# Hymba block on one core: three products of an accumulator in a row in the feature-major projection

## What is computed

```python
h = rms_norm(x, g_mix[l])
p = h @ w_in[l]
aq, ak, av, mq, mk, mv, mo, mi, mf = jnp.split(p, split_idx, axis=-1)
...
qk = jax.nn.silu(causal_dwconv(jnp.concatenate([mq, mk], axis=-1), conv_qk[l]))
...
gates = jnp.concatenate([mi, mf], axis=-1) + b_gates[l]
```

## Time and profile before

| | us |
|---|---|
| median of three runs | 1000.84 |
| lowest and highest run | 1000.76, 1000.9 |
| profiled execution | 1005.44 |
| its span, first to last instruction | 1003.7 |
| TensorE busy in it | 991.8 (99%) |
| VectorE, ScalarE, GpSimd busy | 635.1, 422.7, 668.4 |
| mean granted TensorE clock | 0.995 |

### The profile page before, as it was taken

The page is one execution under the profiler, slowest core; times in us unless marked ns, Lnnn a source line. Parts: engine busy times, 40 slices in busy tenths (PEclk is TensorE's granted clock), DMA queues, the critical chain, the costliest instruction groups (busy, mean ns, idle before and its releaser), DMA issues.

```text
span 1003.7 us, 13162 instructions
## 1 busy us (share of the span) xinstructions
PE 991.8 (99%) x4862; PEld 822.5 (82%) x4862; DVE 635.1 (63%) x777; ACT 422.7 (42%) x868; POOL 668.4 (67%) x529
## 2 busy tenths in 40 slices
PE   9899999999999999999999999999999999999998
PEld 7697788888888888888888888888888888888887
DVE  5259224558862677876748577774748586674585
ACT  6533135547750657524334352434334252433440
POOL 0238056726675516996887786887878788787792
PEclk9999999999999999999999999999999999999999
DMA  8823112141032002112112112112112112211213
GB/s 307 190 75 104 42 43 64 54 147 33 23 126 63 22 11 74 53 42 84 43 42 84 42 43 85 43 42 77 50 42 70 57 42 60 67 42 49 82 59 137
DMA packets 74423, 70.69 MB, mean 70 GB/s; under 512 B 6520, under 2 KB 54776, under 8 KB 74360
## 3 DMA queue, kind: packets, MB, share of 16 engines
q1 hardware_dynamic: 72296, 69.36, 22.6%
q10 hardware_dynamic: 2064, 0.50, 0.3%
HBM read 65.14 MB, written 4.21 MB: 69 GB/s over the span
## 4 chain that ended last, share of the span: by engine, by line
PE 87%; DVE 5%; DMA 3%; SPq 3%; ACT 1%; issue 1%; DVEq 0%; ACTq 0%
PE banks L833 27%; PE banks L835 27%; PE banks L834 27%; DVE qkT L1776 2%; DMA x_in<-in_x 1%; SPq L577 1%; DMA rstd_rows<-rstd 1%; PE banks L1030 1%; PE banks L846 1%; PE banks L927 1%; PE banks L1005 1%; DVE qkT L1774 1%; ACT prob L1541 1%; PE banks L992 1%; DMA rstd_b<-rstd_rows 1%
## 5 line engine op out<-in xcount | busy, mean ns | idle before, releaser
L763 POOL TENSOR_TENSOR wr_lo<-wr_raw,wr_hi 128x512 fp32r<-128x512 f32 x231 | 319.1, 1412 | 27.3 <-ACT wr_hi L1356 22.2
L757 POOL TENSOR_TENSOR wr_raw<-wr_raw,wr_raw 128x512 f32<-128x512 f32 x132 | 193.4, 1469 | 132.2 <-PE banks L835 75.8
L833 PE MATMUL banks<-hf_hi,wr_hi 128*128 128x512 f32 x616 | 240.2, 390 | 0.0
L835 PE MATMUL banks<-hf_hi,wr_lo 128*128 128x512 f32 x616 | 240.0, 390 | 0.0
L834 PE MATMUL banks<-hf_lo,wr_hi 128*128 128x512 f32 x616 | 239.9, 389 | 0.0
L1356 ACT ACTIVATE wr_hi<-wr_raw 128x512 fp32r<-128x512 f32 x231 | 136.7, 625 | 164.8 <-POOL wr_raw L757 107.7
L2177 DVE TENSOR_TENSOR x<-banks,x 128x1024 f32<-128x1024 f32 x138 | 168.8, 1224 | 51.5 <-PE banks L835 35.2
L833 PE MATMUL banks<-w_hi,actT_hi 128*128 128x512 f32 (+1 forms) x384 | 147.9, 385 | 0.0
L835 PE MATMUL banks<-w_hi,actT_lo 128*128 128x512 f32 (+1 forms) x384 | 144.2, 375 | 0.0
L834 PE MATMUL banks<-w_lo,actT_hi 128*128 128x512 f32 (+1 forms) x384 | 144.1, 375 | 0.0
L833 PEld LDWEIGHTS banks<-hf_hi,wr_hi 128*128 128x128 f32 x616 | 115.7, 188 | 24.3 <-issue 0.4
(11 more groups left out here) (205 smaller groups left out, 1201.4 us busy)
## 6 DMA issues: line engine op xcount, KB each, us to landing
wr_raw<-in_w_up SPq DMA_DIRECT2D x46, 256.0 KB, 3.4
wr_raw<-in_w_gate SPq DMA_DIRECT2D x44, 256.0 KB, 3.3
wr_raw<-in_w_down SPq DMA_DIRECT2D x44, 256.0 KB, 3.2
w_raw<-in_w_in SPq DMA_DIRECT2D x32, 256.0 KB, 3.6
x_in<-in_x SPq DMA_DIRECT2D x8, 512.0 KB, 11.6
w_raw<-in_w_out SPq DMA_DIRECT2D x16, 256.0 KB, 2.6
x<-in_x SPq DMA_DIRECT2D x8, 512.0 KB, 5.6
out<-x SPq DMA_DIRECT2D x16, 256.0 KB, 2.1
```

The lines of the kernel that those rows point to most:

```text
L757: nc.gpsimd.tensor_tensor(wr_raw[slot(q, f)][:, :], wr_raw[slot(q, a)][:, :], wr_raw[slot(q, b)][:, :], ALU.subtract).then_inc(wsum, 1)
L763: nc.gpsimd.tensor_tensor(wr_lo[s][:, :], wr_raw[s][:, :], wr_hi[s][:, :].bitcast(F32), ALU.subtract).then_inc(wf_lo, 1)
L833: nc.tensor.matmul(ps, x_hi, wh, start=first, stop=False, skip_group_check=more)
L835: return nc.tensor.matmul(ps, x_lo, wh, start=False, stop=last, skip_group_check=more)
```

## The change

Within a step, the loop over the accumulators becomes the outer one and calls `three` for each, so an accumulator gets its three products of a step in a row. With that all waits of a step stand at its head: `h_split` and, in the first half, `w0_ready`, instead of `h_hi` and `w0_hi` for the first four matmuls and the others further down. The wait for `gains_ready` stays ahead of accumulator 3 of the second half's first step.

```diff
                 for k in range(K):
                     x_hi, x_lo = actT_hi[:, b, k, :], actT_lo[:, b, k, :]
-                    pe.wait_ge(h_hi, K * b + k + 1)
+                    pe.wait_ge(h_split, K * b + k + 1)
                     if b == 0:
-                        pe.wait_ge(w0_hi, k + 1)
+                        pe.wait_ge(w0_ready, k + 1)
                     for f in range(4):
                         if b == 1 and (k, f) == (0, 3):
                             pe.wait_ge(gains_ready, 2)
-                        nc.tensor.matmul(bank[4 * b + f][:, :], w_hi[:, k, f * P:(f + 1) * P], x_hi,
-                                         start=k == 0, stop=False)
-                    pe.wait_ge(h_split, K * b + k + 1)
-                    for f in range(4):
-                        nc.tensor.matmul(bank[4 * b + f][:, :], w_hi[:, k, f * P:(f + 1) * P], x_lo,
-                                         start=False, stop=False)
-                    if b == 0:
-                        pe.wait_ge(w0_ready, k + 1)
-                    for f in range(4):
-                        last = nc.tensor.matmul(bank[4 * b + f][:, :], w_lo[:, k, f * P:(f + 1) * P], x_hi,
-                                                start=False, stop=k == K - 1)
+                        c = slice(f * P, (f + 1) * P)
+                        last = three(bank[4 * b + f][:, :], w_hi[:, k, c], w_lo[:, k, c], x_hi, x_lo,
+                                     k == 0, k == K - 1)
                 last.then_inc(mq_done, 1)
```

## The result

The changed kernel is slower: 1004.03 us median of 7 runs (1003.19 to 1005.53) against 1001.13 us of the kernel before (7 runs beside it, 1000.76 to 1003.77), a ratio of 1.0028 with an interval of 1.0017 to 1.0040. The forecast was 1000.4 us, no change, and 1004.03 lies outside its range.

The account below looks back on a forecast made before the run. TensorE was taken as the bound nearly everywhere; the stage's 1.4 us gain vanishes in the wait at L1083, leaving `nrstd` -0.6 and a cast +0.2: -0.4 us on the 1000.84 median, 1000.4 us, range 998.2 to 1002.6.

Parts of the forecast that it names:

- the base: The profiled execution's 1005.4 us and span of 1003.7 were taken to carry over to the median of 1000.84 as a difference.
- The step that failed second: Before L1083: TensorE's gains, or losses up to 2.3 us, change only its wait there, which grows from 2.3 to 3.7 us.
- Rival 1: Behind L1083 the clock returns sooner, winning 1.9 us more: 998.5 us; chance 0.12.
- The third term: VectorE's chain to `lf`: `nrstd` gains 0.6 us, one more short cast costs 0.2, so `lf` comes 0.4 us earlier.
- The rate: The stage's 192 matmuls: three products in a row into one bank cost the same, a difference of zero.
- The start: First half, step 0: TensorE waits for the low weights and starts at 6.4 us, 0.7 late.
- The wait for the gains: Second half's first step: nine matmuls instead of three stand ahead, so the wait falls from 4.2 to 2.1 us.
- The end of the stage: The edited stage ends at 54.2 instead of 55.62 us, 1.4 earlier, or at 52.7 if the clock is kept.
- The wait for `lf`: TensorE at L1083: expected in the profile after as a wait of 3.2 to 5 us.
- rival 3: Row scales land late behind an earlier weight load, delaying VectorE's chain: up to 1003.5 us; chance 0.08.
- rival 2: The stage's gain counts in full, 1.4 us or 2.9 with the clock kept: 999.4 or 997.9; chance 0.05.
- Rival 4: One or two more GpSimd L694 operations meet VectorE's chain, +0.9 to +1.8 us, up to 1002.2; chance 0.07.

Follow-up runs that it names:

- before_look: The kernel before, unchanged, profiled once more: 999.96 us with a span of 998.2, beside a median of 1000.02 us.
- after_again: The changed kernel with no edit, run and profiled once more: 1001.22 us, ratio 1.0011 to the kernel before.
- early_before: The kernel before, with VectorE copying the gains ahead of its last four `x_low` of the second half: 1003.28 us, ratio 1.0028.
- stage_later: The changed kernel with 13 useless matmuls at the end of the second half, ahead of the signal `mq_done`: 999.9 us, ratio 0.9995.
- all_but_border: The changed kernel with the old order in step 0 of the second half, so 15 of 16 steps in the new order: 1000.74 us, ratio 1.0001.
- border_only: The kernel before with the new order only in step 0 of the second half: 1002.37 us, ratio 1.0009.
- fill_six: The changed kernel with six useless matmuls ahead of the wait for `lf`: 999.96 us, ratio 1.0004.
- fill_after: The changed kernel with 14 useless matmuls ahead of the wait for `lf`: 1000.45 us, ratio 1.0.

## Why the prediction was wrong

Side by side, in us; "before" is the profile nearest to its timed runs (`before_look`), the last two columns the two profiles of the changed kernel. The three were not taken side by side, so an `lf` that moves by a us or two between them need not be the change's doing:

| | before_look | after | after_again |
|---|---|---|---|
| TensorE arrives at L1083 / L1075 | 95.23 | 92.09 | 92.16 |
| `lf` ready | 94.38 | 96.93 | 94.80 |
| wait | 0 | 4.9 | 2.7 |
| lost at 1.2 GHz behind the wait | 0 | 1.7 | 1.7 |
| span | 998.2 | 1001.6 | 999.5 |

**The step that failed first: the base.** The text said of the profiled execution's 1005.4 us that it and its span "both carry over to the median of 1000.84 as a difference". The 4.6 us between the two were not a constant. They were a late `lf` and the half rate behind the wait for it, in that one execution. `before_look` has neither. So the two quantities on which the forecast rested, the wait of 2.3 us at L1083 and the clock of 0.57 behind it, are not part of a typical run of the old kernel. (The row at 33 us varies too: the wait for the gains is 4.2 us there and 2.3 in `before_look`.) The prediction counted 3.4 us of lost clock as common to both orders; the typical old run loses none there, and the two profiles of the new order lose 1.7 us.

**The step that failed second:** "whatever TensorE wins or loses before L1083, up to 2.3 us of loss, changes only how long it waits there". The arrival does change only the wait, but a longer wait can cost clock as well. The clocks of the timed runs show it, since the new order loses nothing at 33 us in any profile and a clock below 1.0 is then lost elsewhere: with 14 or 13 useless matmuls, in 0 of 11 and 0 of 12 runs; with six, in 4 of 11; with none, in 16 of 19; with the arrival earlier still (`early_before`), in 10 of 10. The price in the profiles is 1.7 to 3.4 us. Rival 1 looked at this clock and took it in the wrong direction: a shorter loss, 998.5 us. No rival ended slower by this mechanism. The Trainium skill, "TensorE: Matmul & The Clock Gate", section "What's actually happening", says that the throttled clock is TensorE's default and that activity releases it; the trace agrees (4.9 us idle, then a matmul every 0.43 us instead of 0.23, and 0.23 again from 101.17 us on).

**The third term, not settled:** `lf` was to come 0.4 us earlier. Between the first two profiles it did, by 0.5 us, of which 0.14 are the row scales and 0.36 the chain behind them; but that is a match of two executions that differ for other reasons too. `nrstd` fell from 0.76 to 0.26 (0.15 expected), but the L1766 behind it took 1.78 us against 0.68 in the earlier trace rows, because GpSimd's next L694 met that one instead; what was won there was lost again at once. From the second start of `mq_rows` to the end of `lf` eight profiles whose stage ends early take 35.8 to 37.0 us (mean 36.3), and five whose stage ends late 34.6 to 36.7 (mean 35.6). That suggests a delay of 0.7 us by the change instead of a gain of 0.4. Beside each other on one chip it is clearer: 35.6 against 36.1 to 37.0, 34.6 against 35.8 to 36.3, and 35.3 against 36.7. But the two sets overlap as a whole, the first two profiles go the other way (36.7 and 36.3), and `stage_later` (36.0) did not confirm it. It is likely, and not shown.

**What was right.** The rate: no difference (390 ns, and `all_but_border` at 1.0001). The start: 6.35 for 6.4. The wait for the gains: 1.6 for 2.1. The end of the stage: 52.58, which is the 52.7 named for a kept clock; the text expected the other branch, half rate at 33 us, since a wait of 2.1 was nearest to the 2.3 that had lost clock. The wait for `lf`: 4.9, inside 3.2 to 5. The row scales did not land late (60.58, before 60.72), which takes out rival 3. The chain of rival 2 did not run over the stage. Rival 4's extra meetings exist at most at the 0.7 us above.

**The bill.** From `before_look` to the profile after, TensorE arrives 3.1 us earlier (-3.1), stands 4.9 (+4.9) and loses 1.7 us of clock: 1001.6 - 998.2 = +3.4. The wait does more than take back the lead of 3.1 us: `lf` comes 1.7 us later than TensorE used to arrive. So the clock is half of the difference between these profiles, and the later `lf` the other half; of the 2.6 us by which `lf` is later, 1.5 come from the row scales (60.60 against 59.10) and 1.1 from the chain. How the +2.9 of the medians divides into these two is not known, since the old kernel was profiled in the first comparison only in an execution 4.3 us above its median. In the profile of `after_again` `lf` is 2.1 us earlier, ahead of TensorE's old arrival, and only the clock's 1.7 us are left; nine of its 12 runs lack clock, and the medians give +0.85.

**What stays open.** How much of the loss is a later `lf` and how much the clock. Why `lf` is ready at 96.9 in one profile of the changed kernel and at 94.8 in another: the row scales landed at 60.6 and 59.0 us, a difference of 1.6 in the DMA, but what decides that was not tried. In both profiles of the first comparison VectorE's second `mq_rows` starts at 60.6 or 60.7, in the 13 others at 58.8 to 59.9. What decides whether the clock falls in a wait of 2 to 3 us: 2.3 (the first profile of before), 2.4 (`border_only`) and 2.7 (`after_again`) fell, 2.8 (`fill_six`) did not. At the border of the halves it is the same: the clock fell behind 1.9 us (`all_but_border`, 0.62 from 33 to 37) and not behind 2.2 (`fill_after`, 1.00). Whether the change itself delays `lf`. And what the timed runs of the kernel before at clocks of 0.997 and 0.996 (some 1 us longer than those at 0.998, which lose only the 1.6 us at 33) lose besides: none of them was profiled.

## What to carry to other kernels

Before costing anything, set the profiled execution's time against the median; if it is off by more than the effect you look for, find the difference inside the profile, or read a second execution, before using its waits as terms. Where an engine is made faster ahead of a release that it does not control, the gain becomes a longer wait, and on TensorE a longer wait can cost clock behind it: here 3 us won turned into 2.9 us lost in one comparison and 0.9 in another. Pair such a change with whatever keeps the engine busy or brings the release forward: the same change with the gate one unit later won 0.38%, and with GpSimd's casts one unit later 0.32%.

## What was not expected of the hardware

- Useless matmuls in a wait paid for themselves: 14 of them (3.2 us of work) brought the changed kernel from 1.0028 and 1.0011 times the old one to 1.0.
- Removing a wait of 4.2 us outright (`early_before`) cost 2.9 us.
- A contender on the port matters more by when it runs than by how much. Moving GpSimd's casts by 4.5 us shortened VectorE's chain from 36.3 to 32.5 us. In the same chain one convolution product takes 1.30 us with GpSimd idle and 2.20 to 2.21 with its L694 open, as in the earlier trace rows. The Trainium skill, "SBUF — State Buffer", section "Who interferes with whom", has the two engines exclude each other: the second blocks until the first is through. The 0.9 us of a meeting agree with that, where the prediction read it as the whole 1.29 us of the other operation: in the earlier trace rows the L694 of 65.54 stays open until 67.12, 1.1 us beyond the product's start at 66.00.
- The stage can begin at half rate while the window's mean says otherwise. In `after_again` the granted clock from 6 to 11 us is given as 1.00, yet TensorE in order of time shows a start every 0.43 us, where the first profile of the changed kernel has one every 0.23:

```profile
7.30 0.63 PE L835 MATMUL banks<-actT_hi,w_lo 128*128 128x512 f32 x1
7.73 0.63 PE L833 MATMUL banks<-actT_hi,w_hi 128*128 128x512 f32 x1
8.15 0.63 PE L834 MATMUL banks<-actT_lo,w_hi 128*128 128x512 f32 x1
```

```profile
7.12 0.40 PE L833 MATMUL banks<-actT_hi,w_hi 128*128 128x512 f32 x1
7.36 0.39 PE L834 MATMUL banks<-actT_lo,w_hi 128*128 128x512 f32 x1
7.58 0.39 PE L835 MATMUL banks<-actT_hi,w_lo 128*128 128x512 f32 x1
```

It cost nothing, since the wait for the gains covered it: the transpose came at 30.41 instead of 28.52, and the wait of 1.6 us was gone. `before_look` began this way too, which is why it waits 2.3 us for the gains instead of 4.2: its transpose came at 29.57 instead of 27.70. The distance between starts is the safer reading of the clock.
